# Prompt attentions of a hybrid decoder step: values moved one period later, scores one period earlier

## The chip, the cores and the metric

The program runs on one core of a Trainium2 chip. The metric is the device time of one launch in microseconds (us). The kernel before takes 3481.22 us, the median of 3 runs (3477.48 to 3485.13).

## The reference

The program computes one inference step of two trunk layers for a prompt of 256 tokens and for 8 sequences of 8 new tokens. Each layer is a mixer, an attention to a memory of 256 rows, and a PEER expert layer, each with a residual and a layer norm. The change touches only the attentions of the prompt. There are four of them, and each is a softmax attention of the plain kind. The mixer of layer 0 has two:

```python
# latent attention, 8 heads, 288 wide (256 latent + 32 rotary)
s = einsum('bqhc,bkc->bhqk', q_lat, ckv) + einsum('bqhr,bkr->bhqk', q_rope, krope)
s = where(k_pos <= q_pos, s * MLA_SCALE, -inf)
o_lat = einsum('bhqk,bkc->bqhc', softmax(s), ckv)
# sliding windows, 4 heads of 128, three groups with dilations 1, 4, 16 and a distance bias
o, lse = dilated_group_attend(...)         # per group
o_swa = sum over the groups of softmax(lse) * o
```

The memory attention of each layer is `softmax(q k / 16) v` with 4 heads of 256 over the 256 memory rows.

## The kernel before, in words

The kernel is a sequence of stages. Each stage is one block in which every engine has its own program, engines meet through semaphores, and a barrier (L182) ends it, so that no instruction of a stage starts before all engines, SP with its DMA waits among them, are through with the stage ahead. All data is fp32. A matmul instruction of the source is two instructions in the trace, an fp32 transpose is one.

All four prompt attentions use one helper, `attend_prompt` (L628). It gets a list of units; a unit is one head and one block of 128 queries:

- **mlp** (L1435, L1449): 16 units, 8 heads for each of two query blocks. Scores are three products, two with 128 latent rows and one with 32 rotary rows; 128 keys for the first block, 256 for the second. Two 128x128 outputs.
- **swp** (L1430): 8 units, 4 heads by two blocks; the three window groups side by side, 384 columns for the first block and 768 for the second. One output.
- **m0p, m1p** (L1684, one in each layer): 8 units of 256 columns, two products, two outputs.

In a unit u, TensorE (PE) computes the scores (L664) into PSUM banks 0 and 1 (or 0 to 3), alternating by the parity of u. VectorE (DVE) copies them to SBUF with the mask or bias added (L700, or L703 without), takes the maximum of each row (L705) and scales it (L706). ScalarE (ACT) takes the exponentials with their sum (L735). VectorE takes the reciprocal of the sum (L712) and scales the row (L713). PE transposes the probabilities (L673) into banks 4 and 5, ScalarE copies them to SBUF as `pT` (L747), PE multiplies them with the values (L679) into bank 6 or 7, and VectorE copies the outputs (L719). `s`, `p` and `stat` have two buffers, `pT` has one.

The order on each engine is written out by hand. In period u, PE does scores(u+1), the work beside, transposes(u), values(u). VectorE does finish(u) (L712, L713), maxima(u+1), take(u) (L719). ScalarE does exps(u+1), the work beside, then the copy of `pT` for u.

Work beside comes in with mlp: `BiasByDistance` (L1243) computes 15 chunks of a bias table on PE (L1281) in units 3 to 10, two in a unit and one in unit 10, with 33 rows of 4 columns held and up to 512 columns moved. ScalarE takes each chunk (L1288). SP waits until all 15 are taken, stores the table (L1269), waits for it to land, and issues three DMAs that spread it to 128 rows (L1273); nothing in the stage waits for these three. The stage behind mlp begins with two small loads on SP, the page table (L1472) and a mask (L1473), and a wait for both. In swp, SP stores the windows (L1100 to L1113) and waits for them before the barrier. In m0p and m1p it stores the memory's keys and values in one DMA (L1685) and waits for it.

Of the kernel before, what the change touches and what calls it, by code (L numbers as in the profile page):

```python
# [11 lines left out]
ACT = mybir.ActivationFunctionType  # L12
# [4 lines left out]
P = 128  # L17
# [42 lines left out]
def wait(eng, sem, n):  # L60

    if not isinstance(n, int) or n > 0:
        eng.wait_ge(sem, n)
# [564 lines left out]
def attend_prompt(k, name, units, cols, scale, mask_scales, beside=None):  # L628


    nc = k.nc
    with ExitStack() as ctx:
        s = k.sb(ctx, name + "_s", [P, 2, cols])
        p = k.sb(ctx, name + "_p", [P, 2, cols])
        pT = k.sb(ctx, name + "_pT", [P, cols // P, P])
        stat = k.sb(ctx, name + "_stat", [P, 2, 4])
        scored, s_read, max_ready = k.sem(name + "_scored"), k.sem(name + "_s_read"), k.sem(name + "_max")
        exp_done, p_ready, chain = k.sem(name + "_exp"), k.sem(name + "_p_ready"), k.sem(name + "_chain")
        turned, pT_ready = k.sem(name + "_turned"), k.sem(name + "_pT_ready")
        o_ready, o_taken = k.sem(name + "_o_ready"), k.sem(name + "_o_taken")  # L640
        block = ctx.enter_context(k.block())
        U = len(units)
        psf = k.ps[:, :, :].rearrange("p b n -> p (b n)")
        apart = 512 if cols <= 512 else 1024

        if beside:
            @block.sync
            def _(sp):
                beside.sync(sp)

            @block.gpsimd
            def _(pool):
                beside.gpsimd(pool)

        def width(u):
            return sum(n for _, n, _ in units[u]["scores"])

        @block.tensor
        def _(pe):
            def scores(u):  # L660
                wait(pe, s_read, u - 1)
                for c0, n, prods in units[u]["scores"]:
                    for m, (lhsT, rhs) in enumerate(prods):
                        mm = pe.matmul(psf[:, (u % 2) * apart + c0:(u % 2) * apart + c0 + n], lhsT, rhs,  # L664
                                       start=(m == 0), stop=(m == len(prods) - 1))
                mm.then_inc(scored, 1)

            def values(u):
                pe.wait_ge(p_ready, u + 1)
                wait(pe, pT_ready, u)  # L670
                keys = units[u]["keys"]
                for j, (c0, _) in enumerate(keys):
                    mm = pe.transpose(psf[:, 2048 + j * P:2048 + (j + 1) * P], p[:, u % 2, c0:c0 + P], k.ident[:, :])  # L673
                mm.then_inc(turned, 1)
                pe.wait_ge(pT_ready, u + 1)
                wait(pe, o_taken, u - 1)
                for b in range(len(units[u]["outs"])):
                    for j, (_, vs) in enumerate(keys):
                        mm = pe.matmul(k.ps[:, 6 + u % 2, b * P:(b + 1) * P], vs[b], pT[:, j, :],  # L679
                                       start=(j == 0), stop=(j == len(keys) - 1))  # L680
                mm.then_inc(o_ready, 1)

            scores(0)
            for u in range(U):
                if u + 1 < U:
                    scores(u + 1)
                if beside:
                    beside.tensor(pe, u)
                values(u)

        @block.vector
        def _(dve):
            link = Chain(dve, chain)

            def maxima(u):
                w = width(u)
                src, dst = psf[:, (u % 2) * apart:(u % 2) * apart + w], s[:, u % 2, 0:w]
                dve.wait_ge(scored, u + 1)
                wait(dve, exp_done, u - 1)
                dve.scalar_tensor_tensor(out=dst, in0=src, scalar=mask_scales, in1=units[u]["bias"],  # L700
                                         op0=ALU.mult, op1=ALU.add).then_inc(s_read, 1) \
                    if units[u]["bias"] is not None else \
                    dve.tensor_copy(dst, src).then_inc(s_read, 1)  # L703
                dve.wait_ge(s_read, u + 1)
                link(dve.reduce_max(stat[:, u % 2, 0:1], dst, AX))  # L705
                dve.tensor_scalar(out=stat[:, u % 2, 1:2], in0=stat[:, u % 2, 0:1], scalar1=-scale, scalar2=None,  # L706
                                  op0=ALU.mult).then_inc(max_ready, 1)

            def finish(u):
                w = width(u)  # L710
                dve.wait_ge(exp_done, u + 1)
                link(dve.reciprocal(stat[:, u % 2, 3:4], stat[:, u % 2, 2:3]))  # L712
                dve.tensor_scalar(out=p[:, u % 2, 0:w], in0=p[:, u % 2, 0:w], scalar1=stat[:, u % 2, 3:4],  # L713
                                  scalar2=None, op0=ALU.mult).then_inc(p_ready, 1)

            def take(u):
                dve.wait_ge(o_ready, u + 1)
                for b, dst in enumerate(units[u]["outs"]):
                    last = dve.tensor_copy(dst, k.ps[:, 6 + u % 2, b * P:(b + 1) * P])  # L719
                last.then_inc(o_taken, 1)  # L720

            maxima(0)
            for u in range(U):
                finish(u)
                if u + 1 < U:
                    maxima(u + 1)
                take(u)

        @block.scalar
        def _(act):  # L730
            def exps(u):
                w = width(u)
                act.wait_ge(max_ready, u + 1)
                wait(act, turned, u - 1)
                act.activation(p[:, u % 2, 0:w], s[:, u % 2, 0:w], ACT.Exp, bias=stat[:, u % 2, 1:2], scale=scale,  # L735
                               accum_out=stat[:, u % 2, 2:3]).then_inc(exp_done, 1)

            exps(0)
            for u in range(U):
                if u + 1 < U:  # L740
                    exps(u + 1)
                if beside:
                    beside.scalar(act, u)
                act.wait_ge(turned, u + 1)
                wait(act, o_ready, u)
                nk = len(units[u]["keys"])
                act.activation(pT[:, 0:nk, :].rearrange("p a b -> p (a b)"), psf[:, 2048:2048 + nk * P],  # L747
                               ACT.Copy).then_inc(pT_ready, 1)


def attend_sample(k, name, a):
# [683 lines left out]
def mla_prompt(k, e):  # L1435
    mask = e["mask"]
    units = []
    for qb in range(2):
        n = (qb + 1) * P
        qs = slice(qb * P, (qb + 1) * P)  # L1440
        for h in range(MLA_H):
            prods = [(e["qlatT"][:, c, h, qs], e["ckvT"][:, c, 0:n]) for c in range(2)]
            prods.append((e["qrT"][:, h, qs], e["krT"][:, 0:n]))
            units.append({"scores": [(0, n, prods)], "bias": mask[:, qb, 0:n],
                          "keys": [(kb * P, [e["rows"][:, kb, c * P:(c + 1) * P] for c in range(2)])
                                   for kb in range(qb + 1)],
                          "outs": [e["olatT"][:, c, h, qs] for c in range(2)]})
    with ExitStack() as ctx:
        attend_prompt(k, "mlp", units, SEQ, MLA_SCALE, 1.0, BiasByDistance(k, ctx))  # L1449
# [1005 lines left out]
```

## Time and profile before

| | |
|---|---|
| median of 3 runs | 3481.22 us |
| the profiled execution | 3498.17 us, span 3496.4 us |
| PE busy | 2934.1 us, 84% of the span |
| VectorE busy | 1509.9 us, 43% |
| ScalarE busy | 544.2 us, 16% |
| GpSimd busy | 612.4 us, 18% |
| mean granted TensorE clock | 0.901 of full speed |
| stage mlp | 100.48 to 206.80 us |
| stage swp | 682.40 to 741.10 us |
| stage m0p | 1138.10 to 1181.95 us |
| stage m1p | 2458.35 to 2502.70 us |

The profile is of one execution. Busy times are sums over the whole span, whose larger parts are the two PEER layers, the attentions of the samples and the projections; the four prompt stages are 253 us of 3496. A granted clock of 1.00 is 2.4 GHz, 0.50 is 1.2 GHz. "PEld" is the load of the operand that TensorE holds, "SPq" are DMA issues of SyncE. A wait is put down to the instruction whose semaphore came last.

### The profile page before, as it was taken

The numbers are of one execution on the slowest core, as the hardware profiler recorded it, in microseconds if no ns is written. First come the engines' busy times: TensorE is split into PE (matmuls) and PEld (weight loads), VectorE is DVE, ScalarE is ACT, GpSimd is POOL, SyncE is SP. The second block draws the span as 40 slices with busy tenths as digits, with TensorE's granted clock in tenths as the row PEclk, the third lists the DMA queues.
The fourth block names the chain that finished last, engine by engine and source line by source line (L and its number), as shares of the span: only waits on it lengthen the run. The fifth ranks groups of instructions, "written<-read, shape, count | busy, mean of one in ns | idle before, by whom it ended". The sixth has DMA issues, their size and how long they took to land. (4 is left out here: it accounts for less than half of the span.)

```text
span 3496.4 us, 45163 instructions
## 1 busy us (share of the span) xinstructions
PE 2934.1 (84%) x17313; PEld 2381.8 (68%) x17313; DVE 1509.9 (43%) x3598; ACT 544.2 (16%) x1380; POOL 612.4 (18%) x642
## 2 busy tenths in 40 slices
PE   6867768866669668999989998968678999999997
PEld 3434423554535438999989997644437999989997
DVE  1211100022210225997975553021215997985553
ACT  1223300133301211112100000101221112110000
POOL 0000040000000000433443330000000432443330
PEclk8668889878889789999999999989698999999998
DMA  3349977859842433998989996322343898989995
GB/s 116 108 148 300 316 206 253 280 158 244 206 160 96 162 115 122 355 378 305 348 311 409 409 409 215 121 86 96 121 156 122 318 381 300 349 310 409 408 409 210
DMA packets 275160, 867.70 MB, mean 248 GB/s; under 512 B 30625, under 2 KB 54210, under 8 KB 272423
## 3 DMA queue, kind: packets, MB, share of 16 engines
q1 hardware_dynamic: 198932, 593.14, 48.6%
q0 software_dynamic: 76032, 271.88, 20.6%
q8 instruction: 130, 2.13, 0.3%
q14 instruction: 66, 0.54, 0.0%
HBM read 846.23 MB, written 109.08 MB: 273 GB/s over the span
## 5 line engine op out<-in xcount | busy, mean ns | idle before, releaser
L2271 PE MATMUL ps<-xT,p0e_uT 128*128 128x192 f32 x2048 | 345.9, 328 | 11.1 <-DMA p0e_uT<-in_peer_uT 6.7
L2271 PE MATMUL ps<-xT,p1e_uT 128*128 128x192 f32 x2048 | 345.7, 328 | 9.5 <-DMA p1e_uT<-in_peer_uT 6.4
L2271 PEld LDWEIGHTS ps<-xT,p0e_uT 128*128 128x128 f32 x2048 | 334.0, 191 | 13.9 <-DMA p0e_uT<-in_peer_uT 8.4
L2297 PE MATMUL ps<-p0e_S,p_qT 128*128 128x192 f32 x2048 | 337.3, 327 | 6.3 <-DMA p_qT<-in_peer_v 6.3
L2271 PEld LDWEIGHTS ps<-xT,p1e_uT 128*128 128x128 f32 x2048 | 334.7, 191 | 11.6 <-DMA p1e_uT<-in_peer_uT 7.8
L2297 PE MATMUL ps<-p1e_S,p_qT 128*128 128x192 f32 x2048 | 337.2, 327 | 5.6 <-DMA p_qT<-in_peer_v 5.4
L2297 PEld LDWEIGHTS ps<-p0e_S,p_qT 128*128 128x128 f32 x2048 | 333.1, 190 | 10.4 <-DMA p_qT<-in_peer_v 10.4
L2297 PEld LDWEIGHTS ps<-p1e_S,p_qT 128*128 128x128 f32 x2048 | 332.4, 190 | 10.1 <-DMA p_qT<-in_peer_v 10.0
L2075 DVE SCALAR_TENSOR_TENSOR h_tok<-p1e_rows,p1e_dots,h_tok 128x1024 f32<-128x1024 f32 x127 | 163.1, 1284 | 143.7 <-DMA p1e_rows<-in_peer_v,p1e_expert 125.7
L2075 DVE SCALAR_TENSOR_TENSOR h_tok<-p0e_rows,p0e_dots,h_tok 128x1024 f32<-128x1024 f32 x127 | 163.1, 1284 | 141.3 <-DMA p0e_rows<-in_peer_v,p0e_expert 134.5
L1965 POOL DMA_INDIRECT p0e_rows<-in_peer_u,p0e_expert x128 | 153.4, 1199 | 394.7 <-DVE p0e_dots L2064 207.1
L1965 POOL DMA_INDIRECT p1e_rows<-in_peer_u,p1e_expert x128 | 153.4, 1199 | 393.9 <-DVE p1e_dots L2064 206.9
L1965 POOL DMA_INDIRECT p1e_rows<-in_peer_v,p1e_expert x128 | 127.0, 992 | 195.2 <-DVE h_tok L2075 172.7
L1965 POOL DMA_INDIRECT p0e_rows<-in_peer_v,p0e_expert x128 | 126.1, 985 | 196.4 <-DVE h_tok L2075 174.7
L2064 DVE CUSTOM_DVE_ANT_0 p1e_rows<-p1e_rows,x_tok 128x1024 f32<-128x1024 f32 x128 | 154.9, 1218 | 1.6
L2064 DVE CUSTOM_DVE_ANT_0 p0e_rows<-p0e_rows,x_tok 128x1024 f32<-128x1024 f32 x128 | 154.9, 1218 | 1.6
L844 PE MATMUL ps<-ident,ms_pages 128*128 128x128 f32 (+1 forms) x384 | 70.3, 340 | 64.9 <-DMA ms_pages<-in_cache_mla 60.3
L503 DVE SCALAR_TENSOR_TENSOR x_tok<-x_tok,h_tok 128x1024 f32<-128x1024 f32 (+1 forms) x15 | 17.4, 1218 | 236.9 <-ACT h_tok L471 195.9
L293 PE MATMUL ps<-win_w,xT 128*128 128x512 f32 x192 | 89.9, 630 | 29.3 <-DMA win_w<-in_attn_w_in 29.3
L700 DVE SCALAR_TENSOR_TENSOR swp_s<-ps,e_bias_p 128x384 f32<-128x384 f32 (+1 forms) x8 | 6.1, 757 | 241.2 <-PE ps L664 241.2
L844 PEld LDWEIGHTS ps<-ident,ms_pages 128*128 128x128 f32 (+1 forms) x384 | 48.1, 155 | 86.7 <-DMA ms_pages<-in_cache_mla 37.6
L2288 PE MATMUL ps<-h_tok 128*128 128x128 f32 x768 | 102.6, 276 | 3.3 <-DVE h_tok L2085 3.3
(460 smaller groups left out, 3991.2 us busy)
## 6 DMA issues: line engine op xcount, KB each, us to landing
p_qT<-in_peer_v SPq DMA_DIRECT2D x256, 512.0 KB
p0e_uT<-in_peer_uT SPq DMA_DIRECT2D x128, 512.0 KB
p1e_uT<-in_peer_uT SPq DMA_DIRECT2D x128, 512.0 KB
out_swa_sample<-in_cache_swa_w SPq DMA_DIRECT2D x32, 2040.0 KB, 18.7
m_cache<-in_cache_mem_kv SPq DMA_DIRECT2D x32, 1024.0 KB, 5.8
ms_pages<-in_cache_mla SPq DMA_DIRECT2D x128, 144.0 KB, 2.6
ss_kcache<-in_cache_swa_w SPq DMA_DIRECT2D x72, 256.0 KB, 9.2
ss_vcache<-in_cache_swa_w SPq DMA_DIRECT2D x72, 256.0 KB
```

Of the source, the lines that this page charges most:

```text
L293: mm = pe.matmul(k.ps[0:rows, 4 * s + j, 0:chunk], aT[:, c, t0:t0 + rows], wv[:, c, :], start=(c == 0), stop=(c == kc - 1))
L503: dve.scalar_tensor_tensor(out=k.x[0:n, i, :], in0=k.x[0:n, i, :], scalar=ALPHA, in1=k.h[0:n, i, :], op0=ALU.mult, op1=ALU.add).then_inc(c ...
L700: dve.scalar_tensor_tensor(out=dst, in0=src, scalar=mask_scales, in1=units[u]["bias"], op0=ALU.mult, op1=ALU.add).then_inc(s_read, 1) \
L844: mm = pe.transpose(k.ps[0:w, bank(0, g, slot, G), j * P:(j + 1) * P], src(slot), k.ident[:, :])
L1965: pool.indirect_dma_start(out=gr[:, n % NG, :], out_offset=None, in_=io[table].rearrange("l e d -> (l e) d"), in_offset=bass.IndirectOffse ...
L2064: dve.tensor_tensor_reduce(out=gr[:, n % NG, :], in0=gr[:, n % NG, :], in1=k.x[:, 0, :], scale=1.0, scalar=0.0, op0=ALU.mult, op1=ALU.add, ...
L2075: dve.scalar_tensor_tensor(out=acc, in0=gr[:, (HK + n) % NG, :], scalar=dots[:, n:n + 1], in1=acc, op0=ALU.mult, op1=ALU.add).then_inc(row ...
L2271: mm = pe.matmul(k.ps[:, SB[i % len(SB)], 0:TD], ur[:, i % NU, c, :], k.xT[:, c, D0:T], start=(c == 0), stop=(c == KC - 1))
L2288: mm = pe.matmul(k.ps[:, spread_bank(G), m * P:(m + 1) * P], hotJ[:, G % 2, m, :], hotI[:, G % 2, m, :], start=True, stop=True)
L2297: mm = pe.matmul(k.ps[:, c // 2, c % 2 * TD:(c % 2 + 1) * TD], vr[:, i % NV, c * P:(c + 1) * P], S[:, i, :], start=False, stop=(i == STEPS ...
```

## The change

It reorders the periods of `attend_prompt`, for all four stages. PE does scores(0) and scores(1) first; then period u is values(u-1), transposes(u), scores(u+2), the work beside; values(U-1) comes at the end. VectorE takes the outputs of u-1 in period u, behind maxima(u+1), and those of the last unit at the end. ScalarE copies `pT` of u first, then does exps(u+1), then the work beside. `pT` gets a second buffer, by the parity of u, so its copy waits for values(u-2) and no more for values(u-1).

```diff
-        pT = k.sb(ctx, name + "_pT", [P, cols // P, P])
+        pT = k.sb(ctx, name + "_pT", [P, 2, cols // P, P])
...
-            def values(u):
+            def turn(u):
                 pe.wait_ge(p_ready, u + 1)
                 wait(pe, pT_ready, u)
                 keys = units[u]["keys"]
                 for j, (c0, _) in enumerate(keys):
                     mm = pe.transpose(psf[:, 2048 + j * P:2048 + (j + 1) * P], p[:, u % 2, c0:c0 + P], k.ident[:, :])
                 mm.then_inc(turned, 1)
+
+            def values(u):
+                keys = units[u]["keys"]
                 pe.wait_ge(pT_ready, u + 1)
                 wait(pe, o_taken, u - 1)
                 for b in range(len(units[u]["outs"])):
                     for j, (_, vs) in enumerate(keys):
-                        mm = pe.matmul(k.ps[:, 6 + u % 2, b * P:(b + 1) * P], vs[b], pT[:, j, :],
+                        mm = pe.matmul(k.ps[:, 6 + u % 2, b * P:(b + 1) * P], vs[b], pT[:, u % 2, j, :],
                                        start=(j == 0), stop=(j == len(keys) - 1))
                 mm.then_inc(o_ready, 1)
 
             scores(0)
+            scores(1)
             for u in range(U):
-                if u + 1 < U:
-                    scores(u + 1)
+                if u > 0:
+                    values(u - 1)
+                turn(u)
+                if u + 2 < U:
+                    scores(u + 2)
                 if beside:
                     beside.tensor(pe, u)
-                values(u)
+            values(U - 1)
...
                 finish(u)
                 if u + 1 < U:
                     maxima(u + 1)
-                take(u)
+                if u > 0:
+                    take(u - 1)
+            take(U - 1)
...
             exps(0)
             for u in range(U):
+                act.wait_ge(turned, u + 1)
+                wait(act, o_ready, u - 1)
+                nk = len(units[u]["keys"])
+                act.activation(pT[:, u % 2, 0:nk, :].rearrange("p a b -> p (a b)"), psf[:, 2048:2048 + nk * P],
+                               ACT.Copy).then_inc(pT_ready, 1)
                 if u + 1 < U:
                     exps(u + 1)
                 if beside:
                     beside.scalar(act, u)
-                act.wait_ge(turned, u + 1)
-                wait(act, o_ready, u)
-                nk = len(units[u]["keys"])
-                act.activation(pT[:, 0:nk, :].rearrange("p a b -> p (a b)"), psf[:, 2048:2048 + nk * P],
-                               ACT.Copy).then_inc(pT_ready, 1)
```

## Rows read from the trace of the kernel before

**Rows 1.** Waits of PE, whole run (us in total, times, longest).

```profile
PE ps L679 <- ACT swp_pT L747: 19.4, 8, 3.3
...
PE ps L679 <- ACT mlp_pT L747: 13.6, 16, 1.4
PE ps L679 <- ACT m0p_pT L747: 12.3, 8, 1.8
PE ps L679 <- ACT m1p_pT L747: 12.1, 8, 1.8
```

**Rows 2.** Windows: start:end length, busy us by engine, granted clock, DMA share, GB/s.

```profile
100.48:206.80 106.32, 90.20 (x246) 50.03 (x246) 27.89 (x112) 21.54 (x64) 0.09 (x1) 0.53 0.32 114
682.40:741.10 58.70, 35.62 (x180) 32.38 (x180) 20.37 (x48) 11.34 (x24) 0.00 (x0) 0.68 0.26 72
1138.10:1181.95 43.85, 28.40 (x112) 22.11 (x112) 15.28 (x56) 8.34 (x25) 0.00 (x0) 0.68 0.12 48
2458.35:2502.70 44.35, 29.09 (x112) 22.60 (x112) 15.29 (x56) 8.35 (x25) 0.00 (x0) 0.65 0.12 48
181.09:184.51 3.42, 3.41 (x8) 1.52 (x7) 1.44 (x6) 0.00 (x0) 0.00 (x0) 0.50 0.28 87
1140.24:1143.65 3.41, 0.61 (x3) 0.37 (x4) 1.51 (x6) 1.47 (x5) 0.00 (x0) 1.00 1.00 413
1143.65:1147.07 3.42, 3.42 (x13) 2.95 (x14) 0.91 (x4) 0.00 (x0) 0.00 (x0) 0.50 0.14 58
...
178.90:208.80 29.90, 21.48 (x66) 14.84 (x66) 7.19 (x28) 2.99 (x10) 0.00 (x0) 0.50 0.26 98
```

**Rows 3.** Timeline of m0p: start us, length us, engine, line, operation.

```profile
1138.12 1.97 PE L664 MATMUL ps<-m_kT,m_qT 128*128 128x256 f32 x8 [1.10 <-PEq L182]
...
1139.26 0.42 DVE L703 COPY m0p_s<-ps 128x256 f32<-128x256 f32 x1 [88.56 <-PE ps L664]
...
1140.36 0.51 ACT L735 ACTIVATE m0p_p<-m0p_s,m0p_stat 128x256 f32<-128x256 f32 x1 [0.99 <-DVE m0p_stat L706]
...
1141.00 0.16 DVE L712 RECIPROCAL m0p_stat<-m0p_stat 128x1 f32<-128x1 f32 x1 [0.67 <-ACT m0p_p L735]
...
1141.46 0.42 DVE L703 COPY m0p_s<-ps 128x256 f32<-128x256 f32 x1
...
1159.60 0.97 PEld L679 LDWEIGHTS ps<-m0p_pT,m_mkv 128*128 128x128 f32 x8 [2.08 <-ACT m0p_pT L747]
...
1178.15 0.69 PE L673 MATMUL ps<-ident,m0p_p 128*128 128x128 f32 x2 [1.04 <-DVE m0p_p L713]
```

**Rows 4.** Timeline of swp.

```profile
705.04 2.81 SPq L1113 DMA_DIRECT2D out_swa_sample<-e_kv  x8
...
709.30 0.62 DVE L713 TENSOR_SCALAR swp_p<-swp_p,swp_stat 128x768 f32<-128x768 f32 x1
...
710.92 0.96 DVE L700 SCALAR_TENSOR_TENSOR swp_s<-ps,e_bias_p 128x768 f32<-128x768 f32 x1 [1.00 <-PE ps L664]
...
713.09 0.94 ACT L735 ACTIVATE swp_p<-swp_s,swp_stat 128x768 f32<-128x768 f32 x1 [5.92 <-DVE swp_stat L706]
...
737.83 2.93 PE L679 MATMUL ps<-swp_pT,e_kv 128*128 128x128 f32 x12 [0.90 <-ACT swp_pT L747]
```

**Rows 5.** Timeline around mlp's end: SP, and the next stage's first work.

```profile
171.67 0.28 SPq L1269 DMA_DIRECT2D scratch_bias_by_dist<-bs_by_dist  x1
...
212.66 0.29 POOL L1497 COPY ms_q<-e_qlatT 128x128 f32<-128x128 f32 x1 [112.09 <-POOLq L182]
```

**Rows 6.** Waits of SP from 100 to 215.

```profile
SPq L182 <- DMA ms_mask<-in_causal_new: 4.2, 1, 4.2
```

**Rows 7.** Waits of PE from 100.48 to 171.64.

```profile
PE ps L679 <- ACT mlp_pT L747: 6.6, 10, 1.2
```

**Rows 8.** Timeline of mlp: PE's weight loads.

```profile
180.61 1.40 PEld L664 LDWEIGHTS ps<-e_ckvT,e_qlatT 128*128 128x128 f32 x4
...
183.81 0.29 PEld L673 LDWEIGHTS ps<-ident,mlp_p 128*128 128x128 f32 x2 [0.65 <-issue]
```

## Prediction

> **What bounds the kernel now.** I read the whole-run waits of PE first, because the change only reorders four stages: the prompt attentions mlp (16 units), swp, m0p and m1p (8 units each). PE stands still at the value matmuls (L679) until ScalarE has copied the transposed probabilities (L747): 13.6, 19.4, 12.3 and 12.1 us [rows 1]. No other wait of these stages comes near. The windows over the stages [rows 2] show their lengths, 106.3, 58.7, 43.9 and 44.4 us, with PE busy in 90.2, 35.6, 28.4 and 29.1 of them and VectorE and ScalarE busy in far less. So a chain through several engines sets the pace, not one engine.
>
> The timeline of m0p shows the chain [rows 3]. The scores copy of a unit starts at 1139.26, its exponentials at 1140.36 (1.10 later, the maximum between), the reciprocal of its sum at 1141.00 (0.64 later), and the next unit's scores copy at 1141.46 (0.46 later). In the old order PE does scores(u+1) and transposes(u), VectorE then maxima(u+1), ScalarE exps(u+1) and only then copy(u), which values(u) needs. PE's transposes end early and it waits out that chain, once per unit.
>
> **The clock.** In m0p a stretch with PE busy 0.61 of 3.41 us ended with a fall of the granted clock from 1.00 to 0.50 (2.4 to 1.2 GHz); the next stretch, in which PE never paused, ended with a rise [rows 2]. Over the stages the mean is 0.53 to 0.68. Pauses thus cost twice. In mlp a stretch just as busy, 181.09 to 184.51 with 3.41 of 3.42 us, stayed at 0.50 and brought no rise [rows 2]; the 32-row rotary scores lie in it. So I carry the rises of m0p over to swp and m1p, and not to mlp.
>
> **The change, part by part.**
>
> *Scores two units ahead, copy ahead of the exponentials, values one unit late.* No instruction is added or removed but L747's target. After transposes(u), PE has scores(u+2) to do, then values(u). The chain between transposes(u) and transposes(u+1) is now: copy(u) and exps(u+1) on ScalarE, finish(u+1) on VectorE. VectorE's own round is maxima, exponentials, finish: 1.10 + 0.64 + 0.46 = 2.20 us for 256 columns [rows 3]. For swp's 768 columns: scores copy to exponentials 713.09 - 710.92 = 2.17, exponentials 0.94 + 0.13 (the surplus of 0.64 over 0.51) = 1.07, reciprocal to next scores copy 0.46 + 0.26 = 0.72 (the scaling takes 0.62, in m0p 0.35) [rows 3, 4]: 3.96 us. For its 384 columns I take 2.65, between the two.
>
> *PE's work per unit.* At 2.4 GHz in m0p: 8 value instructions in 0.97, 4 score instructions half of 1.97, two transposes some 0.24 [rows 3]: 2.2 us, a tie with 2.20. I take 2.25. For swp's wide units 12 + 12 + 6 instructions at 0.12 give 3.6, under 3.96. At 1.2 GHz 12 such instructions take 2.93 on the record [rows 4], some 2.5 in a row, so a wide unit has 6.3 and an m0p unit some 3.9: then PE sets the pace and is never idle, which is the state that ended in a rise. So I expect the clock at 2.4 GHz for nearly all of swp, m0p and m1p.
>
> *m0p.* 3.5 us to the first transposes (1138.12 to 1141.00 + 0.60), 7 x 2.25 = 15.8, and a tail of transposes, copy, values and output copy, 3.8 us at 1.2 GHz from 1178.15 to 1181.95 and some 3.1 at 2.4 [rows 3]: 22.4 against 43.8, gain 21.4. *m1p:* the same 22.4 against 44.3, gain 21.9.
>
> *swp.* The clock falls as before at the start, since nothing new runs before the first transposes, some 3.7 us in (m0p's 3.5 and 0.2 for the wider tiles). Then 3 narrow rounds, 8.5 with the slow ones among them, 4 wide rounds 15.8, a tail of 3.7 and 0.8 for stretches at 1.2 GHz: 32.5 against 58.7, gain 26.2. SP issues the window stores beside this stage, the last ones from 705.04 on for 2.81 us [rows 4]; at a DMA share of 0.26 over the stage [rows 2] I take them as landed by 710. The new end is 682.4 + 32.5 = 715, so this cover is thin: what is late next here would be the stores.
>
> *mlp.* PE loses 13.6 us of waits [rows 1] and would be done by about 190 even at 1.2 GHz. But SP works behind PE's side work. The last bias chunk is taken and the by-distance table stored from 171.67 on [rows 5], and then three transfers spread it, 1536 pieces of 2 KB; the DMA share is 0.26, 4 of 16 engines, all through 178.90 to 208.80 [rows 2]. The next stage's small loads stand behind them: the mask's wait is 4.2 us [rows 6], and work starts at 212.66 [rows 5], 41.0 after the last chunk. This distance does not shrink. So the stage gains only what the last chunk gains. Up to it PE waits 6.6 us for ten copies [rows 7]; the transposes' records overstate their length by some 0.25, which adds 2.5: 9.1. Against it, transposes(10) and scores(12) now come ahead of that chunk: 0.4 and 183.81 - 180.61 = 3.2 [rows 8]. That is 5.5 earlier at the same clock. The values, transposes and full-height scores now follow one another without a pause; I give the clock one more fast stretch before the last chunk for it, 2.5: 8.0. Bounds: 3.5 (clock at 1.2 GHz throughout; this run had one fast stretch there) and 13.
>
> On that queue, the Trainium skill ("DMA: Bandwidth & Descriptors", Why a DMA increments its semaphore by 16 and not by 1, and Queues, rings and completion order) says that a transfer is dealt to as many engines as divide its slowest dimension, the lowest-numbered ones, and that each engine takes its descriptors in ring order. Share 0.26 and the mask's late landing agree. Without this rule one might start the next stage some 4 us after PE's end and book 18 for mlp instead of 8; the total would be 3394.
>
> *The new waits.* Copy(u) waits for values(u-2) and values(u) for copy(u), both a whole round old or behind scores(u+2): nothing. Take(u-1) stands ahead of finish(u+1) on VectorE, but values(u-1) is ahead of transposes(u) on PE, so it finds its data; 0.49 of copies fall into the 0.64 of exponentials. At the end of each stage two waits of about 0.5 for copies stay.
>
> Sum: 8.0 + 26.2 + 21.4 + 21.9 = 77.5. The profiled execution took 3498.17 (span 3496.4) and would take 3420.7; it stands 17.0 above the median of the runs, 3481.22, from which I subtract the same: 3403.7.
>
> **Rivals.**
>
> *A, the clock stays mostly at 1.2 GHz.* For: mean clocks of 0.65 to 0.68, and the wait behind the stage's start remains. Against: full stretches of m0p ended in rises. Time: m0p and m1p 3.5 + 7 x 3.9 + 3.8 = 34.6, gain 9.5 each; swp 3.7 + 3 x 3.5 + 4 x 6.1 + 4 = 42.6, gain 16; mlp 3.5: 38.5 in all, 3442.7.
>
> *B, a busy PE is enough for the clock.* mlp would run at 2.4 GHz too. Its last chunk would come at about 139 (half of PE's 64 us of work from 103.6 on at 1.2 GHz, and 3 for what doesn't halve), the next stage at 180: mlp gains 32.6, in all 102, 3379. Against: the stretch from 181.09. The Trainium skill's page "TensorE: Matmul & The Clock Gate" (The two states you'll see) has just this rule, busy means warm; the stretch from 181.09 speaks against it in this form.
>
> *C, slower: the exponentials are the exposed part.* ScalarE now holds exps(u+1) behind copy(u), that is behind transposes(u). If PE found nothing to do in between (scores(u+2) held back by VectorE's read of scores(u), in place of today's cover), each unit would pay its full round of 2.2 or 4.0 behind PE's work instead of today's 1.6 or 3.3 (a stage's wait divided by its units, and the 0.25): 0.6 x 32 + 0.7 x 8 = 25 at most, 22 us more, about 3503. It decides once s_read(u) comes later than transposes(u); in the rows the scores copy ends at 1139.68, 1.9 us ahead of them [rows 3].
>
> *D, it changes nothing:* the copy stays last on ScalarE for another reason. The diff leaves no room for it that I see. 3481.
>
> **Numbers.** The forecast 0.76, A 0.14, B 0.05, C 0.03, D 0.02. The range takes in A and leaves out B's end: 3386 to 3444. A difference of 0.2% (7 us) is about what the runs of this kernel can tell from none: faster 0.95, the same 0.02, slower 0.03.
>
> **What would show it.** Right: the waits at L679 fall to two short ones per stage; rounds of about 2.25 in m0p and 3.96 in swp; granted clock near 1.00 in three of the stages; 41 us from the last chunk to the next stage. Wrong: a mean clock under 0.8 in m0p, a PE wait for probabilities (L673) in every round well above 0.3, swp ending on window stores, or the mask no longer waiting behind the spread.

## The result and the profile after

The changed kernel takes 3394.82 us, the median of 4 runs (3393.15 to 3402.25); the kernel before took 3483.18 us beside it (4 runs, 3477.48 to 3490.60). The ratio is 0.9749, with a 95% interval from 0.9725 to 0.9773: 88.4 us faster by the medians. The prediction was 3403.7 and a gain of 77.5. The profiled execution took 3402.25 us, 95.9 less than that of before.

The head of the page of the changed kernel and its line of busy times:

```profile
span 3400.4 us, 45159 instructions
...
PE 2860.9 (84%) x17313; PEld 2337.6 (69%) x17313; DVE 1509.9 (44%) x3598; ACT 546.1 (16%) x1380; POOL 611.1 (18%) x642
```

VectorE's 1509.9 us is the same to the tenth; PE is busy 73.2 us less with the same work, 58.7 of them inside the four stages. So part of the gain is standing time taken out, and part is PE's own work done at the faster clock. The windows answer to [rows 2], with the same columns. The first four are the stages mlp, swp, m0p and m1p; the last three lie inside mlp and behind its PE work:

```profile
100.70:166.24 65.54, 64.00 (x246) 38.49 (x246) 29.40 (x112) 21.77 (x64) 0.06 (x1) 0.74 0.43 152
665.90:697.15 31.25, 23.96 (x180) 21.91 (x180) 19.82 (x48) 12.04 (x24) 0.00 (x0) 0.95 0.49 135
1088.18:1109.62 21.44, 18.33 (x112) 15.15 (x112) 14.80 (x56) 9.12 (x25) 0.00 (x0) 1.00 0.24 98
2384.37:2405.81 21.44, 18.32 (x112) 15.14 (x112) 14.80 (x56) 9.12 (x25) 0.00 (x0) 1.00 0.24 99
112.60:131.00 18.40, 18.40 (x46) 8.39 (x46) 5.67 (x24) 4.70 (x14) 0.00 (x0) 0.50 0.83 318
134.42:152.85 18.43, 18.43 (x79) 8.99 (x79) 8.89 (x31) 8.14 (x21) 0.00 (x0) 1.00 0.00 0
161.00:192.00 31.00, 3.77 (x28) 3.00 (x27) 2.88 (x12) 1.25 (x4) 0.00 (x0) 0.62 0.26 98
```

Three stages are half as long as before, at a granted clock of 0.95 to 1.00 instead of 0.65 to 0.68. In mlp the stage's own work is through after 65.54 us instead of 106.32, but the next stage's first work on GpSimd begins only at 193.98. For the sum a stage therefore counts from its first PE instruction to the first work of the next stage:

| stage, to the next stage's first work | before | after | gain | predicted |
|---|---|---|---|---|
| mlp | 112.15 | 93.28 | 18.9 | 8.0 |
| swp | 58.93 | 31.54 | 27.4 | 26.2 |
| m0p | 44.07 | 21.72 | 22.3 | 21.4 |
| m1p | 44.59 | 21.72 | 22.9 | 21.9 |
| sum | 259.74 | 168.27 | 91.5 | 77.5 |

The other 4.5 us of the profiled difference lie between the stages, in code that is the same in both kernels. The stretch from swp to m0p alone differs by 6.0, 396.76 us in the profile of before and 390.74 after. That stretch took 369 to 389 us in the profiled executions of the experiments below, with either order of the attentions, so it is no effect of the change.

PE's waits in the four stages, whole run, against [rows 1]. Lines of the source have moved by 3 to 9: L682 is the values (L679 before), L752 the copy of `pT` (L747), L673 the transposes still, L720 the scaling (L713):

```profile
PE ps L673 <- DVE swp_p L720: 5.1, 6, 2.1
PE ps L682 <- ACT swp_pT L752: 1.8, 2, 0.9
PE ps L673 <- DVE m1p_p L720: 1.5, 1, 1.5
PE ps L673 <- DVE m0p_p L720: 1.5, 1, 1.5
PE ps L682 <- ACT mlp_pT L752: 0.9, 2, 0.5
PE ps L682 <- ACT m0p_pT L752: 0.9, 2, 0.5
PE ps L682 <- ACT m1p_pT L752: 0.9, 2, 0.5
```

The waits for the copy of `pT`, 57.4 us over 40 units before, are 4.5 us in eight waits. One wait for the first probabilities stays in swp, m0p and m1p (1.5 to 2.1), and in swp five more of 0.16 to 1.40, the longest where the units go from 384 to 768 columns: there VectorE's round is longer than PE's work.

A round of m0p, by its timeline, against [rows 3]:

```profile
1091.05 0.16 DVE L719 RECIPROCAL m0p_stat<-m0p_stat 128x1 f32<-128x1 f32 x1 [0.67 <-ACT m0p_p L744]
...
1093.25 0.17 DVE L719 RECIPROCAL m0p_stat<-m0p_stat 128x1 f32<-128x1 f32 x1 [0.67 <-ACT m0p_p L744]
...
1093.71 0.42 DVE L710 COPY m0p_s<-ps 128x256 f32<-128x256 f32 x1
1093.85 0.20 PEld L673 LDWEIGHTS ps<-ident,m0p_p 128*128 128x128 f32 x2 [0.19 <-DVE m0p_p L720]
...
1094.02 0.73 PEld L664 LDWEIGHTS ps<-m_kT,m_qT 128*128 128x128 f32 x4
...
1094.78 1.08 PEld L682 LDWEIGHTS ps<-m0p_pT,m_mkv 128*128 128x128 f32 x8
```

From reciprocal to reciprocal is 2.20 us. The transposes wait 0.19 for the scaling; then scores and values follow one another. VectorE's own round sets the pace and PE just keeps up.

The end of mlp, against [rows 5]: SP's issues, then the next stage's first work.

```profile
152.85 0.28 SPq L1278 DMA_DIRECT2D scratch_bias_by_dist<-bs_by_dist  x1
158.30 16.18 SPq L1282 DMA_DIRECT2D scratch_bias_rep<-scratch_bias_by_dist  x3
175.36 8.50 SPq L1481 DMA_DIRECT2D ms_table<-in_page_table  x1
183.91 0.76 SPq L1482 DMA_DIRECT2D ms_mask<-in_causal_new  x1
...
193.98 0.29 POOL L1506 COPY ms_q<-e_qlatT 128x128 f32<-128x128 f32 x1 [93.22 <-POOLq L182]
```

And SP's waits from 95 to 215, against [rows 6]:

```profile
SPq L182 <- DMA ms_mask<-in_causal_new: 8.9, 1, 8.9
SPq L1282 <- DMA scratch_bias_by_dist<-bs_by_dist: 5.2, 1, 5.2
```

The three spreading DMAs occupy SP for 16.18 us in their issue, the small load behind them another 8.50, and the mask then takes 8.9 to land. The stage's own work had ended at 166.24. From the store of the table to the next stage's work is 193.98 - 152.85 = 41.1 us; before it was 41.0. In both kernels the DMA share stays at 0.26 until about 2 us ahead of that work and then drops to 0. The spread ran out at the same distance from the store; before, PE's own work covered most of it.

### The profile page after: what moved, and what is told of

It reads as the page before. It is cut to its first block and busy times, and to the rows that moved or that the text cites. A ratio compares the mean times of both kernels' runs of the same rounds, so it can differ in the third digit from the quotient of the medians.

```text
span 3400.4 us, 45159 instructions
## 1 busy us (share of the span) xinstructions
PE 2860.9 (84%) x17313; PEld 2337.6 (69%) x17313; DVE 1509.9 (44%) x3598; ACT 546.1 (16%) x1380; POOL 611.1 (18%) x642
## 5 line engine op out<-in xcount | busy, mean ns | idle before, releaser
L2280 PEld LDWEIGHTS ps<-xT,p0e_uT 128*128 128x128 f32 x2048 | 335.5, 192 | 17.4 <-DMA p0e_uT<-in_peer_uT 12.1
L853 PEld LDWEIGHTS ps<-ident,ms_pages 128*128 128x128 f32 (+1 forms) x384 | 49.4, 158 | 105.9 <-DMA ms_pages<-in_cache_mla 58.7
L503 DVE SCALAR_TENSOR_TENSOR x_tok<-x_tok,h_tok 128x1024 f32<-128x1024 f32 (+1 forms) x15 | 17.4, 1218 | 235.2 <-ACT h_tok L471 194.9
```

The costliest lines, as they stand in the source:

```text
L503: dve.scalar_tensor_tensor(out=k.x[0:n, i, :], in0=k.x[0:n, i, :], scalar=ALPHA, in1=k.h[0:n, i, :], op0=ALU.mult, op1=ALU.add).then_inc(c ...
L853: mm = pe.transpose(k.ps[0:w, bank(0, g, slot, G), j * P:(j + 1) * P], src(slot), k.ident[:, :])
L2280: mm = pe.matmul(k.ps[:, SB[i % len(SB)], 0:TD], ur[:, i % NU, c, :], k.xT[:, c, D0:T], start=(c == 0), stop=(c == KC - 1))
```

## The experiments

Eleven kernels, in three groups; the kernels of a group ran on one chip with the kernel before beside them (medians 3465.55, 3478.11 and 3476.82 us). The first group's runs of before are spread from 3451.7 to 3492.22, so its small differences are read from stage lengths and not from ratios; the four runs of e2 alone are spread from 3339.94 to 3395.58. Each stage length is from one profiled execution, and those of the old order scatter: e8 leaves swp, m0p and m1p as they were, and there they are 2.8 to 3.5 us shorter than in the profile of before, at clocks of 0.77, 0.78 and 0.74. Stage lengths (to the next stage's first work, us) of all profiled executions:

| kernel | mlp | swp | m0p | m1p | sum | median of runs | ratio to before |
|---|---|---|---|---|---|---|---|
| before | 112.15 | 58.93 | 44.07 | 44.59 | 259.7 | 3483.18 | 1 |
| changed | 93.28 | 31.54 | 21.72 | 21.72 | 168.3 | 3394.82 | 0.9749 |
| e1 | 107.04 | 40.87 | 29.11 | 28.13 | 205.2 | 3414.24 | 0.9846 (0.9775 to 0.9917) |
| e2 | 92.93 | 31.44 | 21.74 | 21.72 | 167.8 | 3383.86 | 0.9703 (0.9593 to 0.9813) |
| e3 | 121.97 | 34.90 | 30.03 | 29.79 | 216.7 | 3438.32 | 0.9910 (0.9877 to 0.9943) |
| e4 | 103.41 | 53.32 | 34.75 | 34.32 | 225.8 | 3437.46 | 0.9918 (0.9884 to 0.9952) |
| e5 | 115.35 | 49.54 | 35.50 | 35.51 | 235.9 | 3443.24 | 0.9891 (0.9864 to 0.9918) |
| e7 | 73.32 | 31.55 | 21.73 | 21.74 | 148.3 | 3368.89 | 0.9683 (0.9661 to 0.9706) |
| e8 | 110.30 | 56.11 | 40.60 | 41.24 | 248.3 | 3474.21, one run | |
| e9 | 64.41 | 31.44 | 21.74 | 21.73 | 139.3 | 3360.95 | 0.9669 (0.9641 to 0.9697) |
| e10 | 92.16 | 31.43 | 21.71 | 21.71 | 167.0 | 3383.39 | 0.9745 (0.9714 to 0.9776) |
| e11 | 93.04 | 31.85 | 21.71 | 21.70 | 168.3 | 3379.96 | 0.9732 (0.9701 to 0.9764) |
| e12 | 62.28 | 31.43 | 21.71 | 21.71 | 137.1 | 3358.05 | 0.9652 (0.9622 to 0.9683) |

### e1: only ScalarE's order

On the kernel before, the copy of `pT` goes ahead of the next unit's exponentials; PE and VectorE keep their order, `pT` its one buffer.

```diff
             for u in range(U):
-                if u + 1 < U:
-                    exps(u + 1)
-                if beside:
-                    beside.scalar(act, u)
                 act.wait_ge(turned, u + 1)
...
                                ACT.Copy).then_inc(pT_ready, 1)
+                if u + 1 < U:
+                    exps(u + 1)
+                if beside:
+                    beside.scalar(act, u)
```

> The kernel before with one edit: ScalarE copies the transposed probabilities of u before the exponentials of u+1. PE's and VectorE's orders, one buffer and the number of scores in advance stay as before. Theory 1 (the exposed part was the exponentials' chain ahead of the copy, and the clock follows the pauses): PE waits only about 0.5 us for the copy in each unit, 0.87 in swp's wide ones, the clock stays near 1.00 in m0p and m1p, and a unit of m0p takes 0.98 scores + 0.25 transposes + 0.5 + 0.9 values, some 2.75 us. Stages: m0p and m1p about 26, swp about 36, mlp earlier by about 5: 3420, that is more than two thirds of the change's gain of 88. Theory 2 (PE's order, values one unit late and scores two ahead, is what matters): less than a third of the gain, 3455 or more, and a mean clock under 0.8 in m0p.

Measured: the stages are 54.6 us shorter, 60% of the change's 91.5. PE's waits at the values and the transposes of e1, whole run:

```profile
PE ps L679 <- ACT mlp_pT L743: 6.7, 16, 0.5
PE ps L679 <- ACT swp_pT L743: 5.9, 8, 0.9
PE ps L673 <- DVE swp_p L713: 4.2, 3, 2.1
...
PE ps L679 <- ACT m1p_pT L743: 3.8, 8, 0.5
PE ps L679 <- ACT m0p_pT L743: 3.8, 8, 0.5
PE ps L673 <- DVE m1p_p L713: 3.6, 8, 1.5
PE ps L673 <- DVE m0p_p L713: 3.4, 7, 1.5
```

The wait for the copy is still there once per unit, but it is now the bare copy, 0.5 us (0.9 for swp), without the exponentials ahead of it. So what PE waited out before was ScalarE's order, which confirms the chain read from [rows 3], and the few lines moved on ScalarE are the largest single part. Both theories missed the size: the first had put it above two thirds and m0p at about 26 us, which took 29.11. It left out a second wait, for the probabilities (L673), some 0.3 us in each further unit of m0p and m1p. The bare copy, this wait, and the clock of 0.67 in mlp and 0.79 in swp (against 0.74 and 0.95) are what scores two ahead and values one late remove.

### e2 and e11: one buffer of transposed probabilities

```diff
-        pT = k.sb(ctx, name + "_pT", [P, 2, cols // P, P])
+        pT = k.sb(ctx, name + "_pT", [P, cols // P, P])
...
-                wait(act, o_ready, u - 1)
+                wait(act, o_ready, u)
```

and `pT[:, j, :]`, `pT[:, 0:nk, :]` where it is read and written.

> The changed kernel with one buffer of transposed probabilities, the copy of u waiting for the values of u-1. Theory 1: those values are ahead of the transposes of u on PE, so the wait is always met: same time as the changed kernel within 0.2%, same stage lengths (m0p 21.7, swp 31.5). Theory 2 (the second buffer carries part of the gain): each unit pays the end of its values, 0.2 to 0.5 us, 8 to 20 us in all.

> The changed kernel with one buffer of transposed probabilities, a second time, since the first comparison's interval was 2.2% wide. Theory 1 (the second buffer carries nothing): the same ratio as the changed kernel beside it, within 0.2%, and stage lengths within 0.5 us. Theory 2: 8 us slower or more.

Measured: 167.8 and 168.3 us of stages against 168.3 and 167.0 with two buffers. Beside e10, the changed kernel on the same chip, e11 is 3.4 us faster by the medians, with ratios to before of 0.9732 and 0.9745 whose intervals overlap. Theory 1 had asked for 0.5 us per stage; mlp differs by 0.9 and swp by 0.4 from e10, and by 0.2 and 0.3 from the first profile of the changed kernel. The second buffer carries nothing that these runs can tell: PE does values(u-1) ahead of transposes(u), so the single buffer is always read before ScalarE has something to write into it.

### e3: outputs taken in the old place

```diff
-                if u > 0:
-                    take(u - 1)
-            take(U - 1)
+                take(u)
```

> The changed kernel with VectorE taking the outputs of u in period u, as before, ahead of the finish of u+1. Theory 1: the values of u now come late on PE, so VectorE waits for them, and the transposes of u+1 wait for take (0.4) and finish (0.6) behind them: about 1.0 us more PE idle in each unit. If the clock stays at 1.00: m0p and m1p about 28, swp about 37, mlp 5 to 15 later, 3420 in all. If the pauses bring the clock down: up to 3455. Theory 2 (VectorE's place of the output copy is indifferent, since VectorE is busy for under half of the time): 3395.

Measured: 48.4 us of the stages' 91.5 are lost, 28.7 of them in mlp, which becomes slower than before (121.97 against 112.15). The window over mlp in e3:

```profile
101.36:212.64 111.28, 94.59 (x246) 52.24 (x246) 26.79 (x112) 22.17 (x64) 0.06 (x1) 0.50 0.30 105
```

and PE's waits of e3, whole run:

```profile
PE ps L673 <- DVE mlp_p L720: 15.1, 15, 1.0
PE ps L673 <- DVE swp_p L720: 9.6, 8, 2.2
PE ps L673 <- DVE m1p_p L720: 8.8, 8, 1.5
PE ps L673 <- DVE m0p_p L720: 8.8, 8, 1.5
```

VectorE now waits for values(u) before finish(u+1), and transposes(u+1) wait for that: a new chain values, take, finish, transposes. It costs 1.0 us a unit, and in mlp the clock stays at 0.50 throughout, which theory 1 had priced at 5 to 15 us and which took 28.7. The profiled execution is the fastest of e3's ten runs (3416.30 us, the median 3438.32), so the stage lengths do not overstate the loss. A reordering on two engines that forgets the third gives back half of what it gained. This is the one way found in which the change could have made a stage slower; its mechanism was not among the rivals.

### e4: scores one unit ahead

```diff
             scores(0)
-            scores(1)
...
-                if u + 2 < U:
-                    scores(u + 2)
+                if u + 1 < U:
+                    scores(u + 1)
```

> The changed kernel with scores one unit ahead: period u is values(u-1), transposes(u), scores(u+1). Theory 1: the round is now transposes, scores, maxima, exponentials, finish, with only the values beside it: 0.25 + 0.98 + 0.2 + 1.10 + 0.64 + 0.60 = 3.8 us in m0p at 2.4 GHz, 4.9 at 1.2 GHz, 6.5 in swp's wide units: m0p and m1p 33 to 41, swp about 46, mlp 10 to 19 later: about 3448, half of the gain or more is lost. Theory 2 (the late values alone cover the copy and that is enough): within 10 us of the changed kernel.

Measured: 57.5 us of the 91.5 are lost. PE's waits of e4, whole run:

```profile
PE ps L673 <- DVE swp_p L719: 18.2, 8, 3.5
PE ps L673 <- DVE m1p_p L719: 11.2, 8, 2.4
PE ps L673 <- DVE m0p_p L719: 11.2, 8, 2.4
PE ps L673 <- DVE mlp_p L719: 10.2, 9, 1.9
```

The foretold chain is there; swp, put at about 46 us, took 53.32. Without the second unit of lead, the wait has only moved from the values to the transposes: in swp 18.2 us in eight waits, against 19.4 for the copies before [rows 1]. This is rival C's loss in its nearest form (PE has nothing to do while the softmax runs), and it does not reach C's price: m0p is 34.75 us, still 9.3 shorter than before.

### e5: the clock alone

On the kernel before, idle PE time ahead of the values is filled with useless 128-row matmuls, in swp, m0p and m1p. The order of the work stays; the wait for the output bank moves ahead of them, in mlp too.

```diff
+                wait(pe, o_taken, u - 1)
+                if name != "mlp":
+                    for _ in range(4 if width(u) > 512 else 2):
+                        pe.matmul(k.ps[:, 6 + u % 2, 0:384], k.ident[:, :], k.x[:, 0, 0:384], start=True, stop=True)
                 pe.wait_ge(pT_ready, u + 1)
-                wait(pe, o_taken, u - 1)
```

> The kernel before, its order untouched, with matmuls of no use (128 rows, 384 columns) in the place where PE waits for the copy in swp, m0p and m1p: two per unit, four in the 768-column units, results overwritten by the values. They show the share of the clock alone. Theory 1 (pauses bring the clock down, and this costs on top of the pauses): the clock is at 1.00 in m0p and m1p and near it in swp, the round is the old chain at 2.4 GHz, 0.9 + 1.0 + 0.1 + 1.10 + 0.64 + 0.41 = 4.15 us in m0p instead of 5.3: m0p and m1p 37, swp some 48 (7.0 in the wide units, 4.1 in the narrow ones), mlp as before: 25 us faster than before. The other 46 of the three stages' 73 us then belong to the order. Theory 2 (the clock makes no difference since the chain through VectorE and ScalarE is what counts): stage lengths within 2 us of before or longer.

Measured, by the windows over swp and m0p:

```profile
686.63:735.89 49.26, 39.89 (x228) 29.74 (x228) 20.18 (x48) 11.34 (x24) 0.00 (x0) 0.97 0.31 86
1108.47:1143.69 35.22, 30.01 (x144) 19.66 (x144) 14.79 (x56) 8.32 (x25) 0.00 (x0) 1.00 0.15 60
```

With the clock at 0.97 to 1.00 and the old order, the three stages gain 9.4, 8.6 and 9.1 us against the profile of before: 27.0 of the 72.6 that the change brings there. Against e8, where the same three stages of the old order took 137.95 us instead of 147.59, the fillers gain 17.4 of 63.0. What does not hang on this choice is the distance from e5 to the changed kernel, 45.6 us, with the clock near 1.00 in both: that is the order. The fillers leave only 0.9 us of waits at the values in m0p, so some of them may lie on the path. So the pauses did cost twice, as the prediction had it: a quarter to three eighths through the clock, the rest directly. Stage mlp, which has no fillers, took 115.35 us here against 112.15, at a clock of 0.55; the runs leave it open whether that is scatter or the moved wait.

### e7 and e8: the spread on 16 engines

The three spreading DMAs of mlp get the 128 rows as their slowest dimension in place of the 4 heads; the same bytes go to the same places. e7 is made on the changed kernel, e8 on the kernel before.

```diff
-            src = bass.AP(io["bias_by_dist"].tensor, g * SWA_H * N_DIST + REP0, [[N_DIST, SWA_H], [0, P], [1, REP_N]])
-            sp.dma_start(io["bias_rep"][g], src).then_inc(k.bias_spread, 16)
+            src = bass.AP(io["bias_by_dist"].tensor, g * SWA_H * N_DIST + REP0, [[0, P], [N_DIST, SWA_H], [1, REP_N]])
+            sp.dma_start(io["bias_rep"][g].rearrange("h p n -> p h n"), src).then_inc(k.bias_spread, 16)
```

> The changed kernel with one edit: the three transfers that spread the bias table have the 128 copies as their slowest dimension instead of the 4 heads. Same bytes. Theory 1 (mlp's end is held by these transfers on 4 of 16 engines, 41 us from the last chunk to the next stage): the DMA share rises from 0.26 to near 1, the transfers take 8 to 12 us instead of 32, the mask's wait falls from 8.9 to about 2 us, and the next stage begins 4 to 7 us after PE's last value: mlp 70 to 73 instead of 93.3, 20 to 23 us faster than the changed kernel. Theory 2 (something else holds SP, its issue of the three transfers for instance, which took 16 us): mlp stays over 85.

> The same edit on the kernel before. Theory 1: there PE ended at 206.8, and the transfers stood only some 2 to 3 us in the way: mlp 109 to 110 instead of 112.15. Theory 2 (the transfers' pace slows everything else in the stage): more than 5 us.

Measured in e7, by SP's issues and the next stage's first work:

```profile
153.60 0.28 SPq L1278 DMA_DIRECT2D scratch_bias_by_dist<-bs_by_dist  x1
159.06 2.70 SPq L1282 DMA_DIRECT2D scratch_bias_rep<-scratch_bias_by_dist  x3
167.41 0.24 SPq L1481 DMA_DIRECT2D ms_table<-in_page_table  x1
...
174.74 0.29 POOL L1506 COPY ms_q<-e_qlatT 128x128 f32<-128x128 f32 x1 [73.26 <-POOLq L182]
```

The next stage starts 21.1 us after the store instead of 41.1, and mlp is 20.0 us shorter, while its own work (65.58) is unchanged. In e8, on the kernel before, mlp is 1.9 us shorter; that is less than such stages scatter, but the mask's wait, 1.4 instead of 4.2, shows the same cause. So the spread was a floor that hardly showed before and that bites only once PE is faster. Windows just behind the issue (same columns as above):

```profile
158.30:170.00 11.70, 7.23 (x46) 5.41 (x45) 5.47 (x21) 2.13 (x7) 0.00 (x0) 0.97 0.78 219
161.00:168.00 7.00, 4.53 (x30) 3.42 (x30) 3.56 (x14) 1.25 (x4) 0.00 (x0) 1.00 0.95 263
```

The DMA share is 0.78, and 0.95 in its middle, instead of 0.26, which is 4 of 16 engines. Theory 1 was too hopeful in the rest: the mask still waits 6.1 us and not about 2, the next stage begins 8 us after PE's last value and not 4 to 7, and mlp takes 73.32. The floor is lower, not gone. The rule of the Trainium skill that the prediction drew on ("DMA: Bandwidth & Descriptors", Why a DMA increments its semaphore by 16 and not by 1) is borne out here by an edit that changes only the order of the dimensions.

### e9 and e12: a warm start in mlp

e7, and four useless matmuls ahead of mlp's first transposes, where PE has nothing else to do for part of the time:

```diff
             scores(1)
+            if name == "mlp":
+                for _ in range(4):
+                    pe.matmul(k.ps[:, 6, :], k.ident[:, :], k.x[:, 0, 0:512], start=True, stop=True)
```

> The kernel of the run before last with four matmuls of no use (128 rows, 512 columns, 3.4 us at 1.2 GHz) ahead of mlp's first transposes, where the clock was at 0.50 for the first 34 us. Theory 1 (a pauseless run of full-height matmuls brings the clock up, and PE's work behind it, without pauses, keeps it up): the clock is at 1.00 from about 107 on, the narrow units take 1.8 instead of 2.94 us, PE's part of mlp ends 8 to 12 us earlier. Theory 3 (the narrow units with their 32-row scores can't keep the clock up): it falls again within a few us and the stage is 1 to 3 us longer.

> The changed kernel with the spread transfers over all engines and four matmuls of no use ahead of mlp's first transposes, beside the changed kernel. Its mlp stage was 64.4 us against 93.3, so 29 us faster than the changed kernel: ratio to the kernel before 0.967.

The useless matmuls of e9, by the timeline, and three stretches of its mlp. The second covers the same microseconds that ran at 0.50 in the changed kernel, with 84 matmul instructions in place of 46; the third is the narrow units' work, from the first transposes to the first scores of 256 columns:

```profile
104.88 5.06 PE L690 MATMUL ps<-x_tok,ident 128*128 128x512 f32 x8
...
107.65:112.60 4.95, 4.95 (x25) 3.22 (x24) 1.55 (x8) 1.43 (x6) 0.00 (x0) 1.00 1.01 376
112.60:131.00 18.40, 18.40 (x84) 9.62 (x85) 10.51 (x45) 8.76 (x26) 0.00 (x0) 1.00 0.88 335
109.78:124.83 15.05, 15.05 (x80) 9.14 (x79) 8.69 (x40) 7.56 (x24) 0.00 (x0) 1.00 1.05 398
```

and the whole of mlp's own work in e12:

```profile
101.35:155.05 53.70, 52.22 (x254) 31.14 (x254) 28.46 (x112) 22.01 (x64) 0.06 (x1) 1.00 0.62 206
```

From the first transposes to the first 256-column scores the changed kernel took 27.6 us (104.55 to 132.13) at 1.2 GHz, and e9 takes 15.05. The stage's own work falls from 65.58 to 56.70 us in e9 and to 53.70 in e12. In e9 the clock was at 0.50 from 100.83 and rose at 107.66, while the useless matmuls ran; in e12 it was at 1.00 from the start and never fell in the stage, so e12 shows that the level holds and not what raises it. In both, PE went on at 2.4 GHz with the small matmuls of the narrow units. The expectation's 3.4 us for the four is what they took at 2.4 GHz (3.53 between their start and the first transposes in e12), and not at 1.2. By whole runs e9 is 7.9 us faster than e7, with intervals that overlap. e12 beats both kernels of the study: 3358.05 us, 0.9652 of before (0.9622 to 0.9683), and 25.3 us under the changed kernel beside it (e10).

### e10: the changed kernel again

The changed kernel as it is, beside e11 and e12.

> The changed kernel as it is, to stand beside the next two on one chip. Ratio to the kernel before 0.975, as first measured.

Measured: ratio 0.9745 (0.9714 to 0.9776) on another chip, where the first result was 0.9749. The stages are within 1.2 us of the first profile.

## Why the prediction was right

**The bound and its cause.** Right, and shown: e1 moves only ScalarE's copy and the waits fall to the bare copy. The two short waits per stage were foretold at about 0.5 and are 0.5 (0.9 in swp).

**The rounds.** Foretold 2.25 and 3.96; m0p has 2.20 and swp's wide reciprocals, at 680.71, 684.66 and 688.62, stand 3.95 apart. Reading VectorE's own round out of the old timeline was good to 2%.

**The clock in three stages.** Right: 0.95, 1.00 and 1.00. That swp's clock falls at the start was right too (0.50 from 670.31 to 673.72), but it does not always do so: in e2, e9, e10 and e12 it stayed at 1.00. The stages are 1.0 to 1.3 us shorter than the prediction had them. In m0p the start was as foretold, 3.48 us to the first transposes; the seven rounds took 15.4 instead of 15.8, and the tail 2.6 instead of 3.1.

**swp's stores.** They do not bind: SP's last issue of the windows ended at 691.3, the DMA share is 0.00 from 692 on, and the stage ended at 697.15.

**mlp.** Here a term was mis-sized. The law was right: 41 us from the last chunk to the next stage, measured as 40.8 to 41.1 in before, changed, e1 to e5, e10 and e11, whatever the rest did, and as 21 to 22 once the spread used 16 engines on the changed order (e7, e9, e12). The error is in when the chunk comes. The table was stored 71.2 us after the stage's first matmul before, and 52.2 after: 19.0 earlier, not 8.0. The step that failed is "I give the clock one more fast stretch before the last chunk for it, 2.5". The row of after is 134.42 to 152.85: PE busy 18.43 of 18.43 us and a clock of 1.00 right up to the store. Up to the store the mean clock was 0.54 before and 0.68 after, that is some 5.5 and 18.4 us at 2.4 GHz; the 12.9 us more could save up to as much again. With the 5.5 us at equal clock as foretold, about 13.5 is left for the clock, so it was worth some 13 and not 2.5, and the stage's gain lies above the upper bound of 13.

**Rival B** was half right. Its claim that a busy PE is enough fails in this kernel: from 112.60 to 131.00 PE never paused and stayed at 1.2 GHz. But mlp did rise, at 134.42, which the prediction had ruled out but for one stretch, and once the clock had risen, narrow units held it, in e9 and e12. The Trainium skill's page "TensorE: Matmul & The Clock Gate" (The two states you'll see) has busy as warm; the row from 112.60 disagrees, and e9's row agrees with it where the clock was already up. What tells the two apart was not isolated. In the five profiles of the changed order without useless matmuls (changed, e2, e7, e10, e11) the rise came 2.0 to 2.4 us behind mlp's first scores of 256 columns, with the 32-row and 33-row operands still among them; in swp it came at 673.72, behind operands of 128 rows and 128 columns only.

**Rival A** (1.2 GHz) fell with the clocks above, and **D** with the result. **C** fell with the waits for probabilities: in m0p 0.19 in a round, and in swp's wide rounds 0.40, close to the 3.96 less 3.6 that the prediction's own sum leaves. The danger that was real and not named is e3's: the place of the output copies on VectorE is worth 48 us of stages.

**The sum.** 14.0 us more than foretold in the stages, 10.9 of them in mlp and 3.1 in the other three; between stages the executions scatter by more than that. The range, 3386 to 3444, held the result. Two things in the nearness are luck. The profiled execution stood 17.0 above the median of before, and that was carried over; after, it stands 7.4 above. And the 3394 that the prediction gives for a kernel without the rule of the spread is what was measured, but by another path: it books 18 us for mlp because nothing would hold the next stage, while here the spread held it for 41.1 us as foretold and the table came 19.0 us earlier.

## What to carry to other kernels

When a pipeline over several engines is reordered, ask for each engine what its queue holds between two links of the chain: one copy moved ahead of the next unit's exponentials was worth 60% of this change, a take left in its old place would have undone half, and the second buffer was worth nothing that the runs could tell. A stage's end has its own law: where a transfer started late in it holds back the next stage's first small loads, PE's gain of 41 us became 19, and giving the transfer all engines by its slowest dimension freed another 20. And work out what a removed pause does to the TensorE clock separately, since a level once reached held here through work that had run at the lower level before.

## What the runs showed of the hardware

- The clock's rise and its hold differ. Narrow units of mlp (32-row and 33-row operands among 128-row ones) left it at 0.50 for 18.4 us of unbroken work in the changed kernel, and the same units kept it at 1.00 for 15.05 us in e9, after four useless matmuls ahead of them. Beside e7, the four brought 8.9 us in mlp's own work in one profile each, their own time paid.
- The layout of a DMA is also a price on the queue that issues it. The three spreading DMAs held SP 15.41 us (before) and 16.18 us (changed) with 4 as their slowest dimension, and 1.95 to 2.70 us with 128, for the same bytes. A page-table load issued 0.9 us behind the former's issue took 8.50 us in its own, and 0.24 in e7, 5.7 us behind the latter's. It took 0.24 in the kernel before too, 14.7 us behind the issue, so how much of the 8.50 is the distance in time was not isolated.
